# Moving weight quarters between attention frames, and fetching gate rows ahead of v, in a hybrid decoder layer on one core

## The reference

```python
h = x @ w_in + b_in
q, k, v, z_b, u, v_a, z_a, g_a, g_b = split(h)           # q, k, v: 3 dilation groups x 8 heads x 128
o_b = merge(attention of each dilation group)            # prompt: causal bands; sample: cached keys and values
y_b = o_b * silu(z_b)
y_a = gelu(u) * (tril(w_s) @ layer_norm(gelu(v_a)) + b_s) * silu(z_a)
merged = sigmoid(g_a) * (y_a @ w_o_a) + sigmoid(g_b) * (y_b @ w_o_b)
out = layer_norm(alpha * x + merged @ w_out)
```

## Time and profile before

| | |
|---|---|
| median of 3 runs | 2413.06 us (2411.82 to 2413.91) |
| the profiled execution: its own time | 2411.71 us |
| its span, first to last instruction | 2410.0 us |
| mean granted TensorE clock | 0.981 |
| PE busy | 2299.5 us, 95% |
| DVE busy | 1611.5 us, 67% |
| ACT busy | 914.2 us, 38% |
| POOL busy | 255.8 us, 11% |

### The profile page before, as it was taken

How to read it: one execution, slowest core, us unless ns; L and a number is a source line. 1 busy time by engine, 2 the same in 40 slices (tenths; PEclk the granted TensorE clock), 3 DMA queues, 4 the chain that set the end, 5 groups by cost and what they waited for, 6 DMA issues and landing times.

```text
span 2410.0 us, 44637 instructions
## 1 busy us (share of the span) xinstructions
PE 2299.5 (95%) x17769; PEld 2251.5 (93%) x17769; DVE 1611.5 (67%) x2124; ACT 914.2 (38%) x1322; POOL 255.8 (11%) x454
## 2 busy tenths in 40 slices
PE   4999999999999999999979989999999979999997
PEld 4999999999999999999978889889889979999996
DVE  7677776777777777777757766676676647553435
ACT  4544444444444444444433323233323332342221
POOL 0000000000000000000023212222221110001000
PEclk8999999999999999999989999999999989999998
DMA  4334334343343343434468757856775563344333
GB/s 150 119 125 132 104 119 131 101 128 117 112 124 116 108 124 113 122 115 135 128 192 254 229 161 220 241 187 202 238 228 164 182 199 120 118 133 125 107 103 114
DMA packets 400460, 357.99 MB, mean 149 GB/s; under 512 B 15787, under 2 KB 359979, under 8 KB 398603
## 3 DMA queue, kind: packets, MB, share of 16 engines
q1 hardware_dynamic: 363168, 206.28, 29.4%
q0 software_dynamic: 37104, 148.95, 19.0%
HBM read 308.75 MB, written 46.41 MB: 147 GB/s over the span
## 4 chain that ended last, share of the span: by engine, by line
PE 82%; DVE 7%; DMA 5%; issue 3%; ACT 2%; SPq 0%; POOL 0%; DVEq 0%; ACTq 0%
PE acc L705 47%; PE acc L759 26%; PE scp L842 3%; DMA raw<-in_w_in 2%; DVE prod L1458 2%; PE scp L827 1%; DVE sc L1483 1%; ACT wh L982 1%; PE turn L779 1%; PE turn L714 1%; DVE far L1459 1%; DMA gbuf<-gate_rows 1%; DMA ones<-in_ones_k 1%; PE scp L794 1%; PE scp L815 1%
## 5 line engine op out<-in xcount | busy, mean ns | idle before, releaser
L705 PE MATMUL acc<-xh,wph 128*128 128x288 f32 x2912 | 868.3, 298 | 38.3 <-DVE wpl L1270 28.7
L705 PE MATMUL acc<-xl,wph 128*128 128x288 f32 x2912 | 860.4, 295 | 0.0
L705 PE MATMUL acc<-xh,wpl 128*128 128x288 f32 x2912 | 857.3, 294 | 0.0
L705 PEld LDWEIGHTS acc<-xh,wph 128*128 128x128 f32 x2912 | 547.1, 188 | 40.7 <-issue 23.2
L705 PEld LDWEIGHTS acc<-xh,wpl 128*128 128x128 f32 x2912 | 549.6, 189 | 0.0
L705 PEld LDWEIGHTS acc<-xl,wph 128*128 128x128 f32 x2912 | 548.2, 188 | 0.0
L1270 DVE TENSOR_TENSOR wl<-raw,wh 128x512 fp32r<-128x512 f32 x256 | 176.9, 691 | 365.6 <-ACT wh L982 365.4
L982 ACT ACTIVATE wh<-raw 128x512 fp32r<-128x512 f32 x256 | 160.9, 629 | 475.5 <-PE acc L759 431.7
L759 PE MATMUL acc<-xh,wh 128*128 128x288 f32 x1024 | 237.2, 313 | 5.1 <-DVE stage L1331 2.9
L759 PE MATMUL acc<-xh,wl 128*128 128x288 f32 x1024 | 221.6, 298 | 0.0
L759 PE MATMUL acc<-xl,wh 128*128 128x288 f32 x1024 | 221.4, 298 | 0.0
(11 more groups left out here) (226 smaller groups left out, 3624.7 us busy)
## 6 DMA issues: line engine op xcount, KB each, us to landing
raw<-in_w_in SPq DMA_DIRECT2D x128, 256.0 KB, 4.7
cache<-in_cache_v POOLq DMA_DIRECT2D x64, 448.0 KB, 5.0
w_a<-in_w_in SPq DMA_DIRECT2D x52, 512.0 KB, 3.8
w_c<-in_w_in SPq DMA_DIRECT2D x52, 512.0 KB, 3.8
w_b<-in_w_in SPq DMA_DIRECT2D x52, 512.0 KB, 3.8
w_d<-in_w_in SPq DMA_DIRECT2D x52, 512.0 KB, 3.9
ones<-in_ones_k POOLq DMA_DIRECT2D x64, 256.0 KB, 3.1
raw<-in_w_out SPq DMA_DIRECT2D x64, 256.0 KB, 2.8
```

The lines of the kernel that those rows point to most:

```text
L705: done = pe.matmul(bank, w[ring][:, k, :], a[x][:, k, :], start=(j in (0, 1, 3, 5) and k == 0 and t == 0), stop=(k == HK - 1 and t == 2), ...
```

## The change

Quarters are dealt 24, 15 (six times) and 14 to the frames. Blocks of four quarters keep their numbers, so they no longer begin where frames begin. In frame 1 attention starts at part 48, at 1.2 parts a step as before; other frames have 1.5 parts a step and the last 1.4. PE's first gate quarter waits for other semaphores. On SP, gate rows 0, 1 and 2 are loaded after branch blocks 0, 1 and 2, and all others one block sooner. POOL fetches v in five parts: three once gate row 0 has landed, two after the first merge; vectors and tables after the second, tg after the third. Heads 0 to 3 of `yb` are rounded and split in the last parts of frame 8, with the low halves kept in turned order. v's statistics and normalisation come in slots 7 to 14.

```diff
-QUARTERS = 16
-PARTS = 64
+QUARTERS = (24, 15, 15, 15, 15, 15, 15, 14)
+AHEAD_PARTS = 48
...
 def part_of(f, step):
-    return 16 + 6 * step // 5 if f == 1 else 8 * step // 5
+    skipped = AHEAD_PARTS if f == 1 else 0
+    return skipped + (parts(f) - skipped) * step // STEPS
...
-                for u in range(QUARTERS):
-                    load(QUARTERS * (f - 1) + u,
-                         quarter_of(w_in, QB * (u % 4), COL_GA + (gate_block(f, u // 4)) * P))
-                    n = gate_block(f, u // 4) - 1
-                    if u % 4 == 3 and n >= 0:
-                        store_gate(n)
+                for u in range(QUARTERS[f - 1]):
+                    q = quarter_no(f, u)
+                    load(q, quarter_of(w_in, QB * (q % 4), COL_GA + q // 4 * P))
+                    if q % 4 == 3 and q > 4:
+                        store_gate(q // 4 - 1)
...
                 branch_block(Q_B, n, w_o_b)
-                if n > 1:
-                    load_gate(n - 2, KB + n - 2)
+                if n < 3:
+                    load_gate(n, KB + n)
+                if n > 3:
+                    load_gate(n - 1, KB + n - 1)
...
-            pool.dma_start(vn[:].rearrange("p c (g d) -> p c g d", g=HEADS),
-                           vn_d.rearrange("g p c d -> p c g d")).then_inc(vn_in, 16)
+            pool.wait_ge(gate_in[0], 16)
+            for c in range(5):
+                pool.dma_start(vn[:, c, :].rearrange("p (g d) -> p g d", g=HEADS),
+                               vn_d.rearrange("g p c d -> p c g d")[:, c, :, :]).then_inc(vn_in, 16)
+                if c in (2, 4):
+                    pool.wait_ge(merged, c // 2)
...
             pool.wait_ge(yb_split, HEADS)
+            pool.wait_ge(merged, 3)
             pool.dma_start(tg[:], tg_d.rearrange("h p t -> p h t")).then_inc(tg_in, 16)
...
-                        if is_at(f, 1) and u < 8:
-                            pe.wait_ge(c_added, 4 * PAIRS_ALL)
-                            pe.wait_ge(pre_split, 1)
+                        if q == 0:
+                            pe.wait_ge(s_copied, 4 * PAIRS_ALL)
+                            pe.wait_ge(c_added, 4 * PAIRS_ALL - 3)
+                            pe.wait_ge(pre_split, 1)
+                        elif q < 8:
+                            pe.wait_ge(c_added, 4 * PAIRS_ALL)
...
+                    if f == HEADS and part in (parts(f) - 5, parts(f) - 3):
+                        act.wait_ge(w_used, Q_B - 2)
+                        act.wait_ge(yb_in, 16)
+                        h0 = part - parts(f) + 5
+                        round_yb(h0, h0 + 2, yb_raw[:, h0:h0 + 2, :])
...
                 if t == 0:
                     read_acc(Q_B, 1, 2 * KB - 1)
-                    act.wait_ge(yb_in, 16)
-                    for h in (0, 2, 4):
-                        round_yb(h, h + 2, yb_raw[:, h:h + 2, :])
+                    round_yb(4, 6, yb_raw[:, 4:6, :])
                     round_yb(6, 7, yb_raw[:, 6:7, :])
...
+                    if f == HEADS and part in (parts(f) - 4, parts(f) - 2):
+                        h0 = part - parts(f) + 4
+                        split_yb(h0, h0 + 2, yb_raw[:, h0:h0 + 2, :])
...
-                    if f == 1 and part == 9:
+                    if f == 1 and part == AHEAD_PARTS - 8:
                         dve.wait_ge(zeroed, 1)
                         spread_queries(0, 64)
-                        for b in range(2):
-                            far_ones(0, b)
+                    if f == 1 and part in (AHEAD_PARTS - 6, AHEAD_PARTS - 3):
+                        far_ones(0, (part - AHEAD_PARTS + 6) // 3)
...
-                if t in (5, 6, 7):
-                    if t == 5:
-                        dve.wait_ge(vn_in, 16)
+                if t in (7, 8, 9):
+                    if t == 7:
+                        dve.wait_ge(vn_in, 80)
...
-                if 9 <= t < 14:
-                    normalise_v(t - 9)
+                if 10 <= t < 15:
+                    normalise_v(t - 10)
```

More of the change, by code:

```diff
@@ L73 @@
 LEAD = RING - 1
-Q_B = HEADS * QUARTERS
+Q_B = sum(QUARTERS)
 Q_A = Q_B + 32
@@ L77, with parts, quarter_no @@
 Q_END = Q_OUT + 64
+def parts(f):
+    return QB * QUARTERS[f - 1]
+def quarter_no(f, u):
+    return sum(QUARTERS[:f - 1]) + u
 def part_of(f, step):
-    return 16 + 6 * step // 5 if f == 1 else 8 * step // 5
+    skipped = AHEAD_PARTS if f == 1 else 0
+    return skipped + (parts(f) - skipped) * step // STEPS
 def slot_qk(i):
@@ L854, in sample_out @@
                     done.then_inc(scored, 1)
-                for part in range(PARTS):
+                for part in range(parts(f)):
                     u, n = divmod(part, QB)
-                    nb = gate_block(f, u // 4)
-                    if n == 0 and u % 4 == 0:
-                        if is_at(f, 1) and u < 8:
+                    q = quarter_no(f, u)
+                    nb = q // 4
+                    if n == 0 and q % 4 == 0:
+                        if q == 0:
[3 more added lines that the diff above has]
+                        elif q < 8:
                             pe.wait_ge(c_added, 4 * PAIRS_ALL)
-                            pe.wait_ge(pre_split, 1)
                         else:
                             pe.wait_ge(acc_read, nb - 1)
-                    quarter(QUARTERS * (f - 1) + u, x_of, range(QB * (u % 4), QB * (u % 4) + QB), (u // 4) % 2, n,
-                            u % 4 == 0, u % 4 == 3)
+                    quarter(q, x_of, range(QB * (q % 4), QB * (q % 4) + QB), nb % 2, n, q % 4 == 0, q % 4 == 3)
                     for s in range(STEPS):
@@ L913, in mix, with y_of @@
                           start=True, stop=True).then_inc(mixed_out, 1)
-            def y_of(hi, lo):
-                return lambda k, h, low: (lo if low else hi)[:, k, h * HALF:(h + 1) * HALF]
+            def y_of(hi, lo, turned_lo=0):
+                return lambda k, h, low: ((lo[:, (k + turned_lo) % HEADS, :] if low and turned_lo else (lo if low else hi)[:, k, :])
+                                          [:, h * HALF:(h + 1) * HALF])
             def branch_block(q0, n, done, hi, lo, split):
@@ L927, in branch_block @@
                             pe.wait_ge(split, QB * v + i + 1)
-                        quarter(q0 + 2 * n + v, y_of(hi, lo), range(QB * v, QB * v + QB), n % 2, i,
+                        quarter(q0 + 2 * n + v, y_of(hi, lo, HEADS // 2 if q0 == Q_B else 0), range(QB * v, QB * v + QB), n % 2, i,
                                 v == 0, v == 1)
@@ L1109, in read_acc, with round_yb @@
                                      bias=bias[:, ds(COL_GA // P + n, 1)]).then_inc(acc_read, 1)
+            def round_yb(h0, h1, src):
+                nc.scalar.activation(ybh[:, h0:h1, :], src, ACT.Copy).then_inc(yb_round, h1 - h0)
             def frame(f, par):
@@ L1146, in round_values @@
                     copy(vh[b % 2][:], cache[:, slot, :, :]).then_inc(v_round, 1)
-                for part in range(PARTS):
+                for part in range(parts(f)):
                     u, n = divmod(part, QB)
-                    q = QUARTERS * (f - 1) + u
+                    q = quarter_no(f, u)
                     if n == 0:
                         ahead(q)
-                        if u % 4 == 0 and not (is_at(f, 1) and u == 0):
-                            read_acc(q, (u // 4 - 1) % 2, gate_block(f, u // 4) - 1)
+                        if q % 4 == 0 and q > 0:
+                            read_acc(q, (q // 4 - 1) % 2, q // 4 - 1)
+                    if f == HEADS and part in (parts(f) - 5, parts(f) - 3):
[3 more added lines that the diff above has]
+                        round_yb(h0, h0 + 2, yb_raw[:, h0:h0 + 2, :])
                     for s in range(STEPS):
@@ L1438, in _, with split_yb @@
             split(1)
+            def split_yb(h0, h1, src):
+                dve.wait_ge(yb_round, h1)
+                at = (h0 + HEADS // 2) % HEADS
+                low(ybl[:, at:at + h1 - h0, :], src, ybh[:, h0:h1, :]).then_inc(yb_split, h1 - h0)
             def frame(f, par):
@@ L1483, in masked @@
                     return v.tensor_tensor_reduce(out, scores, add_, SCALE, MASKED, ALU.add, ALU.max, top_)
-                for part in range(PARTS):
+                for part in range(parts(f)):
                     u, n = divmod(part, QB)
                     if n == 0:
-                        ahead(QUARTERS * (f - 1) + u)
+                        ahead(quarter_no(f, u))
+                    if f == HEADS and part in (parts(f) - 4, parts(f) - 2):
+                        h0 = part - parts(f) + 4
+                        split_yb(h0, h0 + 2, yb_raw[:, h0:h0 + 2, :])
                     if f == 1 and part == 1:
@@ L1648, in _ @@
                 if t == 0:
-                    for h in (0, 2, 4):
-                        split_yb(h, h + 2, yb_raw[:, h:h + 2, :])
+                    split_yb(4, 6, yb_raw[:, 4:6, :])
                     split_yb(6, 7, yb_raw[:, 6:7, :])
```

18 lines of the change are left out of this document (5 added, 13 removed).

## The result

The changed kernel is slower: 2434.64 us (median of 4 runs, 2433.72 to 2436.80) beside 2412.44 for the kernel before (4 runs, 2408.51 to 2413.91). The ratio is 1.0079 (1.0045 to 1.0114); the ratios are estimates over the executions and not quotients of the two medians, which would be 1.0092 here. I had forecast 2399.4 and given slower 0.05. The profiled execution took 2434.61 with a span of 2432.9, 22.9 more than before, where I had a sum of -13.7.

The account below looks back on a forecast made before the run. TensorE, busy almost throughout, was taken as the bound, losing time to waits and low clock. Terms -8.8 + 6.3 - 11.2 = -13.7 took 2411.71 to 2398.0, or 2399.4 as a median; 8-in-10 range 2391 to 2408 us.

Parts of the forecast that it names:

- Frame 1: Attention starting 32 parts later removes the 10.5 us wait on early scores: -8.8 us, bounds -12 to -5.
- Frames 2 to 8: Shorter frames: first turns +6.6, one more clock loss +1.7, covered loads -2.0, together +6.3 us.
- The later turns keep six parts between them: In frames 2 to 8, turns after the first were taken to cost nothing.
- every item keeps its place among the splits: DVE's chain to the first turn stays unshortened, so PE arrives 0.8 us sooner in six frames, 1.6 in the last.
- one more waking: In frames 2 to 8, one extra low-clock stretch after a wait, beside about six today: +1.7 us (0 to +5).
- The branch: At the start of the output branches, old waits and their clock loss go, smaller ones come: -11.2 us.
- head 4's wait of 4.0: First branch block: PE waits 4.0 us (0 to 7) because a weight quarter queues on SP behind `load_gate(0)`.
- my count of DVE's 29.3 us: DVE's work in branch slots 7 to 14, against PE's 28.9 us, makes the first mix wait about 0.8 (0 to 3).
- Rival 1: Branch weight quarter lands unnoticed or the frames' chain finds cover, so waits hardly return: 2388 to 2394 us; chance 0.18.
- Rival 2: Denser frames cost twice: waits near 4 us, each with a longer slow stretch, another 7 us, 2406; chance 0.15.
- Rival 3: In the branch, tables and tg between merges hold SP's gate rows: price 2 to 6 us, 2401 to 2406; chance 0.10.
- Rival 4: Weight load behind `store_gate` meets key, value and query loads in seven frames: 41 us against 8, 2428; chance 0.05.

Follow-up runs that it names:

- The even deal: Changed kernel with 16 quarters in every frame and the first head at part 16 again, branch change kept: 2410.35 us, ratio 0.9991 to the kernel before.
- the deal alone: Kernel before the change with only the new quarters (24, 15 six times, 14) and first head at part 48: 2440.91 us, ratio 1.0122.
- masking first: Changed kernel with DVE masking the last prompt scores before the eighth `far_ones` instead of after it: 2418.41 us, ratio 1.0020 to the kernel before.
- the load-order experiment: Changed kernel with the loads of the first four branch quarters ahead of gate row 0 on SP: 2430.64 us, ratio 1.0069 to the kernel before.
- the tables paced: On the kernel with 20, 16 (six times), 12 quarters, POOL's tables wait for merge 3 and tg for merge 4: 2389.21 us, ratio 0.9890.
- both ends mended: Changed kernel, same quarters, with the first 22 steps of frames 2 to 8 at their old parts, branch loads reordered, v's slots back: 2414.68 us, ratio 0.9999.
- the even one with the same mended branch: Changed kernel with 16 quarters per frame, first four branch quarters loaded ahead of gate row 0, v's slots back at 5 to 13: 2404.01 us, ratio 0.9965.
- the later `far_units`: Each head's first `far_units` after the first normalise, on the 20, 16 (six times), 12 kernel: 2404.61 us; with POOL's tables and tg also delayed: 2401.79 us.

## Why the prediction was wrong

**Frame 1** was right in kind: forecast -8.8 (-12 to -5), measured -5.9. The wait of 10.5 is gone, and the first turn waits 0.4 longer, not 1.7. But late weights cost 4.1 where I had 0.2: PE's waits on `wl` grew from 2.2 to 6.9, where 2.9 of a wait on `stage` went, and loads of 13.7 to 19.7 us, issued from 1303 to 1316, put waits of 1.7 and 0.5 at `pv` and `ss`. The clock gave nothing: of a low stretch of 10.2 us before, 7.3 lay inside the wait of 10.5.

**Frames 2 to 8** failed: forecast +6.3, measured +30.7. The step that failed is this one: "The later turns keep six parts between them (five in frame 8), and normalise 1 now stands ahead of the split it followed, so I cost them at nothing." I had followed DVE's chain to the first turn only and checked the turns after it by their distance from each other. The second `pv` hangs on another chain, from the split of part 24, and that split is tied to PE. What counts is how many parts PE still has from the split to its own need: three and a score product before, one after. Price: six waits of 3.26, 19.6 us. The even deal and the deal alone show that it comes with the deal, and masking first shows it to be DVE's order at this place.

Three smaller errors stand beside it. In frame 8, "every item keeps its place among the splits" was false: a split came in behind ACT's work on the second scores, and the first turn waited 5.46, not 3.8. The waits on `ss` went from 6.6 to 0.6, a gain of 6.0 where I took 2. And the clock: I had one more waking, +1.7, and measured 10.0. The price of one was not the error. Thirteen waits near 3 us and over (twelve in frames 2 to 7, one in frame 8) cost half of 40.1 us, 1.5 each on average; I had left six of them out. But it is no fixed price: four of them cost nothing (frame 2's two, frame 3's first, frame 7's second), four a stretch of 3.4 us and five one of 6.8.

The sum of the miss: 19.6 + 1.7 - 4.0 + 8.3 (clock over forecast) = 25.6, against 30.7 - 6.3 = 24.4 measured.

**The branch** was half right: forecast -11.2, measured -1.5. Both old waits went, and head 4's wait of 4.0 came as 4.33, for the reason given: the load-order experiment takes it down to 0.7. Three terms were mis-sized. The first mix waits 4.5, not 0.8: my count of DVE's 29.3 us let it start in time, but late weights had kept it idle for 3.16 us, until 2003.11, and the slots moved back give 2.5. With the slots back and the tables paced too, the mix waits 0.2. Late weights cost PE 1.0 more. The clock was to give 1.8 and took 2.6: the old slow stretches lay half in PE's waits and cost 3.6, the new ones are full of work, (5.47 + 6.24) / 2 = 5.9. Together 3.7 for the mix, 1.0 for weights, 4.4 of clock, 0.3 for head 4 and 0.3 for a merge are the 9.7 that the branch missed by.

**The rivals.** Rival 1 did not come: the waits that it took away are there. Rival 2 had the longer slow stretches right (6.8 us in five frames), but not the waits that bring most of them. Rival 3 had the right place and cause and the wrong victim: tables and tg hold transfers on SP, gate rows and weights alike, and it was the weights that PE waited for. A `raw` load issued at 1985.11, as POOL's transfers ran, took 10.4 us and the next, at 1988.31, 14.1; those from 2003.83 to 2020 took 2.6 to 3.1. The Trainium skill ("DMA: Bandwidth & Descriptors", Queues, rings and completion order) has the engines take turns between queues, packet by packet. My estimate of twice a quiet load's time, about 6, took the turns to be of equal size, and the measurement decides against that estimate, not against the page: from 1988.3 to 2002.4 the trace has 934 packets of POOL's queue with 3.61 MB and 2114 of SP's with 1.30 MB, 3.9 KB against 0.6 KB each. Rival 4, the slower one, came near (2428 against 2434.6) by luck, for another reason than the one I gave; its own terms, 41 less 8 on 2399.4, even make 2432. Its mechanism, late weights in the frames, cost PE 0.3 us in frames 2 to 8 of the changed kernel. It shows where the front of the frames is as before: there the waits of PE that follow within 3 us on a wait of ACT for `raw` come to 11.4 us in four frames, and to 16.9 in six with both ends mended.

**What stays open.** Why a load takes 17 us in one frame and 3 in the next, at the same place of the list, and why the deal with 15 quarters is 10 us slower than the even one with the same mended branch (2414.7 against 2404.0, two series) although frame 1's wait of 9.5 is gone. In its profiled execution late weights put waits of 4.1 and 5.5 into that frame instead. But the profiled executions of the two, 2409.7 and 2414.0, lie the other way round than the medians and can't settle it. No run set the POOL bursts of the frames apart from the weight loads. The 5 to 13 us that the later `far_units` cost is seen as waits at `pv` and late weights but not worked out.

## What to carry to other kernels

When a schedule is made denser, list every place where the busiest engine takes something from another, and for each count the distance from the last item that is tied to the busiest engine's own progress (here a split) to the place of need, not only the distance between the needs. In an in-order queue, put what the busiest engine needs next ahead of background work of the same step: one swap in DVE's list was worth 16 us. And space out background transfers: with a deal that leaves the full frames as they were, and with loads in order of need, this change's ideas made the kernel 1.1% faster instead of 0.8% slower.

## What the runs showed of the hardware

- In frames 4 to 6 of the changed kernel two waits of 2.9 and 3.3 us, 18.4 us apart, go with a granted clock of 0.50 for 3.4 and then 6.8 us; with the deal alone the same two waits, 19.5 us apart, go with 6.8 and then 3.4. Where the second is 0.87 (the last scores masked first) the clock stays at 1.00 behind it. In frame 2 of the changed kernel the same pair brings nothing, and in frames 3 and 7 one stretch each, so a wait has no fixed price. Over the whole execution the same matmuls were busy for 2312.9 us instead of 2299.5, as section 1 of its profile page says:

```profile
PE 2312.9 (95%) x17769; PEld 2265.3 (93%) x17769; DVE 1609.3 (66%) x2124; ACT 913.6 (38%) x1322; POOL 256.0 (11%) x458
```

- A 256 KB weight load takes 2.6 to 3.1 us alone and 10 to 25 us in a burst of POOL's transfers. Many such loads cost PE nothing: in frames 2 to 8 of the changed kernel six loads took 10.6 to 13.2 us, and no wait of PE over 0.3 follows from them. Elsewhere the wait of PE behind one is up to 6.4 us, in other frames from one kernel to the next.
